# Feed-forward of an encoder layer: two passes instead of one, and the first sequence's up projection as seven block products

## The chip, the cores and the metric

One core of one Trainium2 chip runs the whole program in one launch. The metric is device time in microseconds (us), the median of three runs: 2488.31 us for the kernel before (2484.97 to 2488.56). TensorE is PE in the profile (PEld its weight loads), VectorE is DVE, ScalarE is ACT, GpSimd is POOL, SyncE is SP and issues the DMAs.

## The reference, cut to what matters

Two sequences (1024 and 512 tokens, model width 1024) go through the same encoder layer: attention, cross attention, and the gated feed-forward network, which alone is changed. All data are fp32.

```python
D_FF = 2816
h = _rmsnorm(x, norm_ffn_g)
u = jnp.einsum('bsd,df->bsf', h, w_up)              # width 2 * 2816
up = jnp.pad(u, ((0, 0), (1, 1), (0, 0)))
u = up[:, :-2] * conv_w[0] + up[:, 1:-1] * conv_w[1] + up[:, 2:] * conv_w[2] + conv_b
a, b = jnp.split(u, 2, axis=-1)
x = x + jnp.einsum('bsf,fd->bsd', jax.nn.silu(a) * b, w_down)
return _rmsnorm(x, final_norm_g)
```

## The kernel before, in words

Every operand of a matmul is held as two halves of type fp32r: `hi` (the value rounded) and `lo` (the rest). A product is three matmuls, hi by hi, hi by lo and lo by hi, each of 128x128 stationary by 512 moving columns. So each weight is split by POOL in two steps, a TENSOR_SCALAR that writes hi (L1683) and a TENSOR_TENSOR that subtracts (L1685), and each activation by ACT (hi) and DVE (lo).

The last phase, `rest_phase`, runs the output projection, the cross attention, its output projection, and from 1384.5 us of the span the feed-forward. Its steps up to there are in an order that a planner (`rest_plan`) writes out from costs and due times. The feed-forward is a loop over 22 groups of 128 hidden channels (`groups`, with `body` on each engine; a group has a gate unit s = 0 and a value unit s = 1). All 1536 tokens go together: the three chunks of 512 tokens of unit s fill three PSUM banks (`up_bank`), 8 k-steps of three matmuls each (`up`, L1719). `woven` lays the 24 down products of the group before (`down`, L1852, two banks `down_bank`) between the up products of the same iteration: a list of (up, down) steps that PE and DVE both follow. DVE adds each down product onto the rows `x` (`add`, L2081).

The up product of a unit is read out of PSUM in place: ACT applies the middle tap and the bias (L1957), DVE the two shifted taps (`conv_part`, L2071, one input in PSUM), ACT the silu (L1961), DVE the product of gate and value (L2102), ACT its hi half (L1963), DVE its lo half (L2104). Weights come by SP (`load`, L1598) into one staging buffer per kind. The last group is cut into three chunks (`END_PARTS`), and its down products are merged with those of the group before (L1894), followed by the final norm of each row tile (L2125, L1999, L2129, L1709, then L1990 and L1705, or L2137) and the stores.

## Time and profile before

| | kernel before |
|---|---|
| median of 3 runs | 2488.31 us |
| the profiled execution, whole | 2487.8 us |
| its span in the trace | 2486.0 us |
| mean granted TensorE clock | 0.995 |
| PE busy | 2432.8 us (98%) |
| DVE busy | 1477.4 us (59%) |
| POOL busy | 904.9 us (36%) |
| ACT busy | 823.2 us (33%) |

Busy is the union of the times in which an engine has an instruction in flight. A matmul of 512 columns is in flight for 0.39 us, but the next one starts much sooner, so the work of PE is read from the distance between starts, not from durations. The 1.8 us between the profiled execution and its span lie around the program.

### The profile page before, as it was taken

What the parts mean: (1) busy time and instruction counts of PE and PEld (TensorE: products, weight loads), DVE (VectorE), ACT (ScalarE), POOL (GpSimd) and SP (SyncE); (2) the same over time, 40 slices, a digit from 0 to 9 for tenths busy, and PEclk for the clock granted to TensorE, in tenths of its full rate; (3) what the DMA queues carried; (4) which work ended last, traced back from release to release, by engine and by line L of the source; (5) the groups of instructions that cost most, each with busy time, mean ns of one, the idle gap of its engine ahead of it and who ended that gap; (6) DMA issues with size and microseconds to landing.
All of it is one profiled execution on the core that took longest, in us unless ns stands there. A gap on an engine that the chain in (4) does not pass through costs nothing.

```text
span 2486.0 us, 34448 instructions
## 1 busy us (share of the span) xinstructions
PE 2432.8 (98%) x12666; PEld 2100.7 (85%) x12666; DVE 1477.4 (59%) x2149; ACT 823.2 (33%) x1498; POOL 904.9 (36%) x1234
## 2 busy tenths in 40 slices
PE   7999999999999989999999999999999999999997
PEld 6999999998998878888888888888888888888886
DVE  7536666788889963333434355555555555555555
ACT  4335555555778841133322211111111111111114
POOL 5453645598878520242400221122122212121223
PEclk9999999999999999999999999999999999999999
DMA  8743434432212162211434401010001100110102
GB/s 298 240 171 124 154 136 157 155 134 98 76 62 82 32 203 85 93 68 60 144 117 138 186 26 34 25 42 28 31 25 42 34 25 28 40 34 25 34 26 102
DMA packets 83379, 224.60 MB, mean 90 GB/s; under 512 B 8000, under 2 KB 43200, under 8 KB 72768
## 3 DMA queue, kind: packets, MB, share of 16 engines
q1 hardware_dynamic: 81968, 222.69, 26.0%
q8 instruction: 70, 1.15, 0.2%
q10 hardware_dynamic: 1296, 0.39, 0.1%
q14 instruction: 45, 0.37, 0.0%
HBM read 174.82 MB, written 48.23 MB: 90 GB/s over the span
## 4 chain that ended last, share of the span: by engine, by line
PE 63%; DVE 1%; issue 0%; POOL 0%; DMA 0%; ACT 0%; POOLq 0%; SPq 0%; DVEq 0%; ACTq 0%
PE r_bank L1719 29%; PE r_bank L1852 13%; PE r_bank L1748 11%; PE r_bank L1781 5%; PE r_bank L1894 1%; PE r_bank L1800 1%; PE r_bank L1829 1%; PE r_bank L1763 1%; PE r_bank L1812 0%; DVE r_x_rows L2137 0%; DMA o_raw<-o_scratch 0%; POOL r_w_lo L1685 0%; DVE r_prob L2051 0%; POOL r_w_hi L1683 0%; DVE r_conv L2119 0%
## 5 line engine op out<-in xcount | busy, mean ns | idle before, releaser
L2081 DVE TENSOR_TENSOR r_x_rows<-r_bank,r_x_rows 128x512 f32<-128x512 f32 x480 | 331.0, 690 | 356.8 <-PE r_bank L1852 356.8
L1719 PE MATMUL r_bank<-r_h_hi,r_w_hi 128*128 128x512 f32 x1056 | 411.0, 389 | 1.2 <-POOL r_w_lo L1685 1.2
L1719 PE MATMUL r_bank<-r_h_lo,r_w_hi 128*128 128x512 f32 x1056 | 410.8, 389 | 0.0
L1719 PE MATMUL r_bank<-r_h_hi,r_w_lo 128*128 128x512 f32 x1056 | 410.8, 389 | 0.0
L1683 POOL TENSOR_SCALAR r_w_hi<-r_stage 128x1024 fp32r<-128x1024 f32 x63 | 66.5, 1055 | 800.0 <-PE r_bank L1852 486.7
L832 PE MATMUL t_proj<-t_w_hi,t_hbuf 128*128 128x384 f32 x1056 | 311.1, 348 | 0.7 <-DVE t_hbuf L1075 0.5
L1957 ACT ACTIVATE r_conv<-r_bank,r_tap 128x1536 f32<-128x1536 f32 x42 | 68.8, 1637 | 630.7 <-PE r_bank L1719 630.7
L1719 PEld LDWEIGHTS r_bank<-r_h_hi,r_w_hi 128*128 128x128 f32 x1056 | 198.2, 188 | 42.7 <-POOL r_w_lo L1685 1.6
L1719 PEld LDWEIGHTS r_bank<-r_h_hi,r_w_lo 128*128 128x128 f32 x1056 | 198.2, 188 | 41.2
L1719 PEld LDWEIGHTS r_bank<-r_h_lo,r_w_hi 128*128 128x128 f32 x1056 | 198.2, 188 | 41.1
L1129 DVE TENSOR_REDUCE t_max_neg<-t_scores 128x1 f32<-128x1024 f32 (+1 forms) x192 | 197.7, 1037 | 33.2 <-PE t_scores L863 32.6
L996 ACT ACTIVATE t_prob<-t_scores,t_max_neg 128x1024 f32<-128x1024 f32 (+1 forms) x192 | 187.2, 976 | 67.9 <-DVE t_max_neg L1129 64.1
L2071 DVE SCALAR_TENSOR_TENSOR r_conv<-r_bank,r_tap,r_conv 128x1023 f32<-128x1023 f32 (+1 forms) x168 | 167.8, 1010 | 57.3 <-ACT r_conv L1957 55.7
L832 PEld LDWEIGHTS t_proj<-t_w_hi,t_hbuf 128*128 128x128 f32 x1056 | 196.3, 190 | 3.5 <-issue 0.7
L1149 DVE TENSOR_TENSOR t_pt_lo<-t_turn,t_pt_hi 128x512 fp32r<-128x512 f32 x240 | 163.1, 685 | 47.2 <-ACT t_pt_hi L1005 44.7
L1852 PE MATMUL r_bank<-r_w_hi,r_g_hi 128*128 128x512 f32 x480 | 188.7, 393 | 1.3
L1852 PE MATMUL r_bank<-r_w_lo,r_g_hi 128*128 128x512 f32 x480 | 186.8, 389 | 0.0
L1852 PE MATMUL r_bank<-r_w_hi,r_g_lo 128*128 128x512 f32 x480 | 186.8, 389 | 0.0
L832 PE MATMUL t_proj<-t_w_lo,t_hbuf 128*128 128x384 f32 x528 | 178.9, 339 | 0.0
L1005 ACT CAST t_pt_hi<-t_turn 128x512 fp32r<-128x512 f32 x240 | 139.4, 587 | 97.8 <-PE t_turn L876 85.3
L1685 POOL TENSOR_TENSOR r_w_lo<-r_stage,r_w_hi 128x1024 fp32r<-128x1024 f32 x63 | 151.6, 2406 | 5.3
L876 PE MATMUL t_turn<-ident,t_prob 128*128 128x128 f32 x960 | 142.8, 274 | 5.7 <-DVE t_ms L1156 2.4
(234 smaller groups left out, 5154.6 us busy)
## 6 DMA issues: line engine op xcount, KB each, us to landing
t_hbuf<-split_x SPq DMA_DIRECT2D x60, 1024.0 KB, 4.8
r_stage<-in_w_up_units SPq DMA_DIRECT2D x44, 512.0 KB, 3.3
split_x<-t_hbuf SPq DMA_DIRECT2D x12, 1024.0 KB, 4.9
r_stage<-in_w_down SPq DMA_DIRECT2D x22, 512.0 KB, 3.3
t_stage<-in_w_in_units SPq DMA_DIRECT2D x6, 1536.0 KB, 7.0
t_xkv_raw<-in_w_xkv_heads SPq DMA_DIRECT2D x16, 512.0 KB, 6.4
t_x_raw<-in_x_turned SPq DMA_DIRECT2D x12, 512.0 KB, 8.3
h_raw<-mix_scratch SPq DMA_DIRECT2D x12, 512.0 KB, 8.2
```

The lines of the kernel that those rows point to most:

```text
L832: ins = nc.tensor.matmul(proj_bank(i), l, r[:, k, :], start=(k == 0 and j == 0), stop=(k == KT - 1 and j == 2))
L876: ins = nc.tensor.transpose(ps_t[:, slot, kk * 2 * P + qt * P:kk * 2 * P + (qt + 1) * P], prob[:, n % PSLOTS, keys], ident[:, :])
L996: nc.scalar.activation(prob[:, n % PSLOTS, 0:p.keys], ps_s[:, n % 2, 0:p.keys], ACT.Exp, bias=max_neg[:, n % COLS:n % COLS + 1], accum_out ...
L1005: nc.scalar.copy(pt_hi[:, n % 2, :], ps_t[:, slot, :]).then_inc(pthi_done, 1)
L1129: nc.vector.tensor_reduce(max_neg[:, n % COLS:n % COLS + 1], ps_s[:, n % 2, 0:p.keys], AX.X, ALU.max, negate=True).then_inc(max_done, 1)
L1149: nc.vector.tensor_tensor(pt_lo[:, n % 2, :], ps_t[:, slot, :], f32(pt_hi[:, n % 2, :]), ALU.subtract).then_inc(ptlo_done, 1)
L1685: nc.gpsimd.tensor_tensor(w_lo[s][:, :], stage[s][:, :], f32(w_hi[s][:, :]), ALU.subtract).then_inc(w_split[s], 1)
L1719: ins = nc.tensor.matmul(up_bank(s)[:, c * BANK:(c + 1) * BANK], l, r, start=(k == 0 and j == 0), stop=(k == KT - 1 and j == 2))
L1748: ins = nc.tensor.matmul(acc(t)[:, cols], l[:, k, :], r[:, cols], start=(k == 0 and j == 0), stop=(k == KT - 1 and j == 2))
L1852: ins = nc.tensor.matmul(down_bank(n), l, r, start=j == 0, stop=j == 2)
L2071: ins = nc.vector.scalar_tensor_tensor(conv[:, s, o], up_bank(s)[:, x_cols], tap[:, j, s:s + 1], conv[:, s, o], ALU.mult, ALU.add)
L2081: nc.vector.tensor_tensor(x[:, t, cols], down_bank(n), x[:, t, cols], ALU.add).then_inc(add_done, 1)
```

## The change

The feed-forward runs in two passes over the 22 groups.

First pass: the second sequence (512 tokens, "sample") alone. A group has 8 + 8 up products (one bank for each unit) and 8 down products; on PE the gate unit runs alone and the value unit is interleaved with the downs of the group before. In groups 1 to 4 DVE also forms sums of blocks of the first sequence's normed activations (`sum_step`), in groups 5 to 11 ACT and DVE split the seven block operands into halves (`low_step`), between the adds.

Second pass: the first sequence (1024 tokens, "prompt"). The up product of a group is a 2x2 by 2x2 block product: gate and value unit by halves of the model width on the weight side, halves of the width by the two chunks of 512 tokens on the other. Instead of eight block products of 4 k-steps it has seven, `w11, s2, s1, w12, s3, w22, s4`, in the Strassen-Winograd form. POOL forms the sums of weight blocks (5 sums of 512 columns per group) and splits seven weight operands of 512 columns and two halves of the down weight. Out of the products DVE forms the four results with four adds in which one input is a PSUM bank; they lie in SBUF (`value`, `gate`), so the shifted taps now have both inputs in SBUF. The gate's second chunk comes out last (product s4), so the gated activations are made in two parts: the first 384 tokens (`edge`) and, in the next group's time, the other 640 (`late`). The 16 downs of the group before are interleaved with products 3 to 6; down 0 waits for `edge_split`, down 3 for `late_split`. Group 21's downs are merged with group 20's at the end, as before.

Around it: the output projection of the cross attention takes its row tiles in another order (`XO_TILES`), so that the second sequence's tiles are ready earlier, and DVE makes no lo half for the first sequence's tiles. Everything is unrolled; the loop and its `tap` copies are gone. Loads of weight quarters are 256 KB instead of 512 KB. The diff, cut to its core:

```diff
--- before.py
+++ after.py
...
+PRODUCTS = ("w11", "s2", "s1", "w12", "s3", "w22", "s4")
+PARTNER = {"w11": "h11", "s2": "t2", "s1": "t1", "w12": "h21", "s3": "t3", "w22": "t4", "s4": "h22"}
+PRODUCT_BANK = {"w11": 2, "w12": 2, "s2": 3, "s3": 3, "s1": 0, "s4": 0, "w22": 1}
...
+XO_TILES = [0, 1, 2, 3, 8, 9, 10, 11, 4, 5, 6, 7]
...
+EDGE = 3 * P
+SUMS = 4
...
+            def halves(hi, lo, raw):
+                stepped(nc.gpsimd.tensor_scalar(hi[:, :], raw[:, :], 1.0, 1.0, ALU.mult, ALU.mult))
+                return nc.gpsimd.tensor_tensor(lo[:, :], raw[:, :], f32(hi[:, :]), ALU.subtract)
...
+            def s3_of(i):
...
+                slot_free(i, "s3", "s3")
+                raw = wop_raw["s3"]
+                stepped(nc.gpsimd.tensor_tensor(raw[:, :], w_rows["w11"][:, :], w_rows["w21"][:, :], ALU.subtract))
+                halves(wop_hi["s3"], wop_lo["s3"], raw).then_inc(op_ready, 1)
...
+            def s2_s1_of(i):
...
+                slot_free(i, "s2", "w22")
+                s1, s2 = wop_raw["s1"], wop_raw["s2"]
+                stepped(nc.gpsimd.tensor_tensor(s1[:, :], w_rows["w21"][:, :], w_rows["w22"][:, :], ALU.add))
+                nc.gpsimd.tensor_tensor(s2[:, :], s1[:, :], w_rows["w11"][:, :], ALU.subtract).then_inc(s2_summed, 1)
+                pool.wait_ge(s2_summed, i + 1)
+                halves(wop_hi["s2"], wop_lo["s2"], s2).then_inc(op_ready, 1)
+                halves(wop_hi["s1"], wop_lo["s1"], s1).then_inc(op_ready, 1)
...
+            def s4_of(i):
+                pool.wait_ge(op_done, done_at(i, "w12"))
+                raw = wop_raw["s4"]
+                nc.gpsimd.tensor_tensor(raw[:, :], w_rows["w12"][:, :], f32(wop_hi["s2"][:, :]), ALU.subtract).then_inc(s4_begun, 1)
+                pool.wait_ge(s4_begun, i + 1)
+                stepped(nc.gpsimd.tensor_tensor(raw[:, :], raw[:, :], f32(wop_lo["s2"][:, :]), ALU.subtract))
+                halves(wop_hi["s4"], wop_lo["s4"], raw).then_inc(op_ready, 1)
...
+            for i in range(1, FT):
+                if i < LAST:
+                    split(i + 1, 0)
+                split_down(i, 0)
+                if i < LAST:
+                    split(i + 1, 1)
+                split_down(i, 1)
...
+            for i in range(FT):
+                from_rows(i, "w22")
+                if i == 0:
+                    pool.wait_ge(s_mean, ST)
...
+                s4_of(i)
+                if i < LAST:
+                    from_rows(i + 1, "w11")
+                    s3_of(i + 1)
+                    s2_s1_of(i + 1)
+                    if i == 0:
+                        from_rows(i + 1, "w12")
+                        down_half(i, 0)
                     else:
...
+                        down_half(i, 0)
+                        from_rows(i + 1, "w12")
+                    down_half(i, 1)
...
+            for i in range(1, FT):
+                for k in range(KT):
+                    sample_up(i, 0, k)
+                for k in range(KT):
+                    sample_up(i, 1, k)
+                    sample_down(i - 1, k)
...
+                if k == 0:
+                    pe.wait_ge(op_ready, ready_at(i, name))
+                    if name == "w11":
+                        pe.wait_ge(*((c11_out, i) if i else (y_done, both)))
+                        if i == 0:
+                            pe.wait_ge(h_op_done, HK * len(H_OPERANDS))
+                    elif name == "s2" and i:
+                        pe.wait_ge(u_done, i)
+                    elif name == "s1":
+                        pe.wait_ge(*((c12_done, i) if i else (s_conv_done, 2 * LAST + 1)))
+                    elif name == "w12":
+                        pe.wait_ge(p1_out, i + 1)
+                    elif name == "s3":
+                        pe.wait_ge(v_done, i + 1)
+                    elif name == "w22":
+                        pe.wait_ge(*((c21_done, i) if i else (s_conv_done, 2 * FT)))
+                    elif name == "s4":
...
+            def prompt_down(i, n):
+                c, t = n // PTILES, n % PTILES
+                if t == 0:
+                    pe.wait_ge(wd_ready, 2 * i + c + 1)
+                    pe.wait_ge(edge_split, i + 1)
+                elif n == 3:
+                    pe.wait_ge(late_split, i + 1)
+                if P_DOWNS * i + n >= 4:
+                    pe.wait_ge(p_add, P_DOWNS * i + n - 3)
+                elif n == 0:
+                    pe.wait_ge(s_add, S_DOWNS * FT)
+                tile = slice(t * P, (t + 1) * P)
+                three(down_bank(n), g_hi[:, tile], g_lo[:, tile], wd_hi[c][:, :], wd_lo[c][:, :], True, True).then_inc(p_down, 1)
...
+            for i in range(FT):
+                for o, name in enumerate(PRODUCTS):
+                    for k in range(HK):
+                        product(i, name, k)
+                        if i == 0 and o == 2:
+                            sample_down(LAST, 2 * k)
+                            sample_down(LAST, 2 * k + 1)
+                        elif 0 < i < LAST and 2 <= o < 6:
+                            prompt_down(i - 1, HK * (o - 2) + k)
...
+                    act.wait_ge(c21_done, i + 1)
+                    mid(i, 1, whole, value[:, :], value_mid)
+                    act.wait_ge(edge_prod, i + 1)
+                    if i == LAST:
+                        act.wait_ge(op_done, done_at(LAST, "w11"))
+                    elif i:
+                        act.wait_ge(p_down, P_DOWNS * i)
+                    else:
+                        act.wait_ge(y_sent, 16 * ST)
+                    nc.scalar.copy((e_hi if i == LAST else g_hi)[:, edge], conv[:, 0, edge]).then_inc(edge_hi, 1)
...
+                for n in range(S_DOWNS if i else 0):
+                    if i == 1 and n == 0:
+                        dve.wait_ge(s_rows_loaded, 16 * ST)
+                        dve.wait_ge(h_hi_done, both)
+                    sample_add(i - 1, n)
+                    if n % 2 and 1 <= i <= SUMS:
+                        sum_step(i - 1, n // 2)
+                    elif n % 2 and SUMS < i <= SUMS + len(H_OPERANDS):
+                        low_step(i - SUMS - 1, n // 2)
+                sample_shifts(i, 1)
...
+            def gated(i, cols, silu, prod, hi_done, split_done):
+                dve.wait_ge(silu, i + 1)
+                dve.wait_ge(value_conv, i + 1)
+                nc.vector.tensor_tensor(conv[:, 0, cols], conv[:, 0, cols], conv[:, 1, cols], ALU.mult).then_inc(prod, 1)
+                dve.wait_ge(hi_done, i + 1)
+                hi, lo = (e_hi, e_lo) if i == LAST else (g_hi, g_lo)
+                nc.vector.tensor_tensor(lo[:, cols], conv[:, 0, cols], f32(hi[:, cols]), ALU.subtract).then_inc(split_done, 1)
...
+            for i in range(FT + 1):
+                if i:
+                    dve.wait_ge(op_done, done_at(i - 1, "s4"))
+                    dve.wait_ge(v_done, i)
+                    nc.vector.tensor_tensor(gate[:, second], one_bank(PRODUCT_BANK["s4"]), gate[:, second], ALU.add).then_inc(c12_done, 1)
+                    dve.wait_ge(late_mid, i)
+                    two_shifts(i - 1, 0, (slice(BANK, 2 * BANK), slice(BANK - 1, 2 * BANK - 1)),
+                               (slice(BANK - 1, 2 * BANK - 1), slice(BANK, 2 * BANK)), late_conv)
+                else:
+                    for n in range(S_DOWNS):
+                        sample_add(LAST, n)
+                if i < FT:
+                    dve.wait_ge(p1_out, i + 1)
+                    dve.wait_ge(op_done, done_at(i, "s2"))
+                    if i:
+                        dve.wait_ge(late_conv, i)
+                    nc.vector.tensor_tensor(gate[:, second], one_bank(PRODUCT_BANK["s2"]), value[:, second], ALU.add).then_inc(v_done, 1)
+                if i:
+                    gated(i - 1, rest, late_silu, late_prod, late_hi, late_split)
+                else:
...
+                if i < FT:
...
+                    prompt_adds(i - 1, 0, 10)
+                    dve.wait_ge(c11_out, i + 1)
+                    two_shifts(i, 0, (slice(1, BANK), slice(0, BANK - 1)), (slice(0, BANK - 1), slice(1, BANK)), edge_conv)
+                    if i == 0:
...
+                        dve.wait_ge(s_rstd, 1)
+                        sample_scale(0)
+                    prompt_adds(i - 1, 10, 11)
+                    dve.wait_ge(op_done, done_at(i, "s3"))
+                    if i:
+                        dve.wait_ge(value_conv, i)
+                    nc.vector.tensor_tensor(value[:, first], one_bank(PRODUCT_BANK["s3"]), value[:, second], ALU.add).then_inc(u_done, 1)
+                    dve.wait_ge(u_done, i + 1)
+                    dve.wait_ge(v_done, i + 1)
+                    nc.vector.tensor_tensor(value[:, second], one_bank(PRODUCT_BANK["s1"]), value[:, first], ALU.add).then_inc(c22_done, 1)
+                    if i == 0:
+                        for t in range(1, ST):
+                            sample_scale(t)
+                    prompt_adds(i - 1, 11, 15)
+                    dve.wait_ge(op_done, done_at(i, "w22"))
+                    dve.wait_ge(c22_done, i + 1)
+                    nc.vector.tensor_tensor(value[:, first], value[:, first], one_bank(PRODUCT_BANK["w22"]), ALU.subtract).then_inc(c21_done, 1)
+                    prompt_adds(i - 1, 15, 16)
+                    dve.wait_ge(value_mid, i + 1)
+                    two_shifts(i, 1, (slice(1, 2 * BANK), slice(0, 2 * BANK - 1)), (slice(0, 2 * BANK - 1), slice(1, 2 * BANK)), value_conv)
+                    gated(i, edge, edge_silu, edge_prod, edge_hi, edge_split)
...
```

## Rows read from the trace of the kernel before

**Rows 1.** The page, parts 1 and 4: busy times, and the chain by engine.
```profile
PE 2432.8 (98%) x12666; PEld 2100.7 (85%) x12666; DVE 1477.4 (59%) x2149; ACT 823.2 (33%) x1498; POOL 904.9 (36%) x1234
...
PE 63%; DVE 1%; issue 0%; POOL 0%; DMA 0%; ACT 0%; POOLq 0%; SPq 0%; DVEq 0%; ACTq 0%
```

**Rows 2.** Timeline of PE: start us, us, then the instruction; its first and two mid-loop ups.
```profile
1384.54 0.39 PE L1719 MATMUL r_bank<-r_h_hi,r_w_hi 128*128 128x512 f32 x1
...
2001.41 0.39 PE L1719 MATMUL r_bank<-r_h_lo,r_w_hi 128*128 128x512 f32 x1
...
2004.13 0.39 PE L1719 MATMUL r_bank<-r_h_lo,r_w_hi 128*128 128x512 f32 x1
```

**Rows 3.** Waits from 1350 us on: who waited for whom, us in total, times, longest.
```profile
PEld r_bank L1852 <- issue: 9.2, 19, 0.5
...
PE r_bank L1894 <- DVE r_x_rows L2125: 3.0, 1, 3.0
```

**Rows 4.** Groups by line and shape: busy us, mean ns of one, idle before.
```profile
L2081 DVE TENSOR_TENSOR r_x_rows<-r_bank,r_x_rows 128x512 f32<-128x512 f32 x480 | 331.0, 690 | 356.8 <-PE r_bank L1852 356.8
...
L2071 DVE SCALAR_TENSOR_TENSOR r_conv<-r_bank,r_tap,r_conv 128x1023 f32<-128x1023 f32 x84 | 107.3, 1277 | 56.5 <-ACT r_conv L1957 55.7
...
L2071 DVE SCALAR_TENSOR_TENSOR r_conv<-r_bank,r_tap,r_conv 128x511 f32<-128x511 f32 x84 | 62.3, 742 | 0.8
...
L2027 DVE SCALAR_TENSOR_TENSOR r_normed<-r_x_xo,r_stat,r_gain 128x1024 f32<-128x1024 f32 x12 | 15.4, 1286 | 8.0 <-POOL r_stat L1632 8.0
```

**Rows 5.** Single lines of POOL and ACT: duration ns min/median/max, first and last start.
```profile
L1663 POOL TENSOR_SCALAR wxo_hi<-wxo_raw x16: 617/618/664, 1200.7 to 1232.7; 128x512 fp32r<-128x512 f32 x16
...
L1666 POOL TENSOR_TENSOR wxo_lo<-wxo_raw,wxo_hi x16: 1277/1288/1302, 1201.4 to 1233.4; 128x512 fp32r<-128x512 f32 x16
...
L1957 ACT ACTIVATE r_conv<-r_bank,r_tap x42: 1636/1637/1637, 1402.1 to 2403.9; 128x1536 f32<-128x1536 f32 x42
...
L1976 ACT ACTIVATE r_conv<-r_bank,r_tap x6: 762/780/781, 2415.5 to 2438.0; 128x512 f32<-128x512 f32 x6
...
L1982 ACT ACTIVATE r_conv<-r_conv x3: 524/633/740, 2417.9 to 2435.0; 128x512 f32<-128x512 f32 x1, 128x384 f32<-128x384 f32 x1, 128x640 f32<-128x640 f32 x1
...
L1985 ACT CAST r_e_hi<-r_conv x3: 512/622/724, 2421.6 to 2441.3; 128x512 fp32r<-128x512 f32 x1, 128x384 fp32r<-128x384 f32 x1, 128x640 fp32r<-128x640 f32 x1
```

**Rows 6.** Single lines of DVE, both inputs in SBUF, in the same form.
```profile
L2011 DVE TENSOR_TENSOR o_lo<-o_raw,o_hi x12: 1220/1226/1226, 1237.9 to 1366.5; 128x1024 fp32r<-128x1024 f32 x12
...
L2102 DVE TENSOR_TENSOR r_conv<-r_conv x21: 1759/2330/2336, 1424.1 to 2409.8; 128x1536 f32<-128x1536 f32 x21
...
L2145 DVE TENSOR_TENSOR r_conv<-r_conv x3: 558/692/826, 2420.9 to 2440.5; 128x512 f32<-128x512 f32 x1, 128x384 f32<-128x384 f32 x1, 128x640 f32<-128x640 f32 x1
```

**Rows 7.** Timeline of POOL and DVE where such an operation meets a split.
```profile
2013.68 2.41 POOL L1685 TENSOR_TENSOR r_w_lo<-r_stage,r_w_hi 128x1024 fp32r<-128x1024 f32 x1
...
2015.37 2.33 DVE L2102 TENSOR_TENSOR r_conv<-r_conv 128x1536 f32<-128x1536 f32 x1
```

**Rows 8.** Timeline of DVE and POOL, 909 to 919 us, several in a row.
```profile
910.00 5.95 DVE L2011 TENSOR_TENSOR h_lo<-h_raw,h_hi 128x1024 fp32r<-128x1024 f32 x3
...
909.79 1.29 POOL L1645 TENSOR_TENSOR r_wxq_lo<-r_wxq_raw,r_wxq_hi 128x512 fp32r<-128x512 f32 x1
911.05 1.60 POOL L1642 TENSOR_SCALAR r_wxq_hi<-r_wxq_raw 128x512 fp32r<-128x512 f32 x1
912.73 2.13 POOL L1645 TENSOR_TENSOR r_wxq_lo<-r_wxq_raw,r_wxq_hi 128x512 fp32r<-128x512 f32 x1
914.84 1.59 POOL L1642 TENSOR_SCALAR r_wxq_hi<-r_wxq_raw 128x512 fp32r<-128x512 f32 x1
```

**Rows 9.** Stretches at the end: busy us by engine, granted clock, DMA; and the chain's last matmuls.
```profile
2445.00:2449.00 4.00, 4.00 (x12) 3.11 (x11) 1.45 (x3) 1.07 (x3) 0.55 (x1) 0.57 0.00 0
...
2443.68 32.70 PE r_bank L1894 x132
```

**Rows 10.** DMA issues by line: KB each, median us to landing.
```profile
r_stage<-in_w_up_units SPq DMA_DIRECT2D x44, 512.0 KB, 3.3
```

More of the change, by code:

```diff
@@ new lines, in rest_phase, with ready_at @@
+        edge_hi, late_hi, edge_split, late_split = sem("edge_hi"), sem("late_hi"), sem("edge_split"), sem("late_split")
+        p_rows_loaded, p_down, p_add = sem("p_rows_loaded"), sem("p_down"), sem("p_add")
+        last_gain, end_down, end_add, sum_done = sem("last_gain"), sem("end_down"), sem("end_add"), sem("sum_done")
+        last_mean, last_rstd, scaled, out_a, out_b, y_sent = (sem(n) for n in ("last_mean", "last_rstd", "scaled", "out_a", "out_b", "y_sent"))
+        def ready_at(i, name):
+            late = ("w22", "s4")
+            if name in late:
+                return NP * i + 6 + late.index(name)
+            return NP * i + 1 + (("w11", "s3", "s2", "s1", "w12") if i else ("w11", "s2", "s1", "w12", "s3")).index(name)
@@ L1612, in _ @@
[L1612 to L1618 removed]
+                        sp.wait_ge(pv_done, EB * XU)
+                    elif s == 2:
+                        for e in range(EB):
+                            sp.wait_ge(o_stored[CH - 1][e], 16 * X_HEADS)
@@ new lines, in three, with sample_down @@
+            def three(out, l_hi, l_lo, r_hi, r_lo, first, last, onto=False):
+                for j, (l, r) in enumerate(((l_hi, r_hi), (l_hi, r_lo), (l_lo, r_hi))):
+                    ins = nc.tensor.matmul(out, l, r, start=(first and j == 0), stop=(last and j == 2), skip_group_check=onto)
+                return ins
+            def sample_down(i, n):
+                t, c = n % ST, n // ST
+                if t == 0:
+                    pe.wait_ge(w_split[2], 2 * i + c + 1)
+                    pe.wait_ge(s_split, i + 1)
+                    if i == 0:
+                        pe.wait_ge(h_hi_done, both)
+                if S_DOWNS * i + n >= 4:
+                    pe.wait_ge(s_add, S_DOWNS * i + n - 3)
+                tile, cols = slice(t * P, (t + 1) * P), slice(c * BANK, (c + 1) * BANK)
+                three(down_bank(n), sg_hi[:, tile], sg_lo[:, tile], w_hi[2][:, cols], w_lo[2][:, cols], True, True).then_inc(s_down, 1)
```

670 lines of the change are left out of this document (393 added, 277 removed).

## Prediction

> **What bounds the kernel now.** I read the busy times and the chain first. PE is busy 98% of the span and holds 63% of the chain that ended last, every other engine 1% or less [rows 1]. Then the timeline of PE in the loop: 12 matmuls, from 2001.41 to 2004.13, take 2.72 us, so one takes 0.2267 [rows 2]. PE's part of the feed-forward runs from 1384.54 [rows 2] to 2443.68 + 32.70 = 2476.38 [rows 9], that is 1091.8 us. It holds 22 x (144 up + 72 down) = 4752 matmuls, 1077.2 us. The other 14.6 us are a wait of 3.0 before the last downs, 1.3 lost at the lower clock behind it (12 matmuls in 4.00 us instead of 2.7; granted clock 0.57, partly 1.2 GHz), the turns of the loop, where the weight load stood 9.2 us in 19 places [rows 3, 9], and small things. So this stage is matmuls back to back, and a matmul less is 0.2267 us less as long as everything else keeps up. The question is whether it does.
>
> **The matmuls.** After, a group has 48 + 24 for the second sequence and 7 x 4 x 3 = 84 products and 48 downs for the first: 204 instead of 216. 22 x 12 x 0.2267 = **59.8 us less**, 4488 matmuls in 1017.4 us. The unrolled program also drops the turns of the loop; of the 14.6 us I leave 4 standing.
>
> **What one shape costs.** POOL at 512 columns: hi 0.62, a subtraction or sum 1.29 [rows 5]. DVE: add out of PSUM 0.69; a shift 0.74 at 512 columns and 1.28 at 1023; product or lo half 0.83 at 640 and 0.56 at 384 [rows 4, 6]. ACT: tap and bias 0.78 at 512, 1.64 at 1536, so 1.21 at 1024; silu 0.74 and 0.52, hi half 0.72 and 0.51 at 640 and 384 [rows 5]. From the end of one engine's step to the next engine's start I take 0.04, and 0.2 from PE's nominal end.
>
> **POOL's load.** First-sequence group: 9 splits (1.91 each) and 5 sums (1.29) are 23.6 us, with 14 gaps of 0.08 behind a wait 24.7. PE has 132 matmuls, 29.9 us. Before it was three splits of 1024 in 49 us. DVE has 21 adds out of PSUM, 14.5, and ten operations with both inputs in SBUF: six shifts (4 x 0.74 + 2 x 1.28) and four of product and lo (2 x 0.83 + 2 x 0.56), 8.3 us. Each engine alone fits under 29.9.
>
> **But these ten and POOL exclude each other.** L2102, both inputs in SBUF, takes 1.76 at least but 2.33 in the median [rows 6]; it starts at 2015.37 while a POOL subtraction lasts until 2016.09, and ends 1.61 after that: it waited and gained only 0.15 by overlap [rows 7]. Several in a row alternate strictly: from POOL's end at 911.08 to DVE's third end at 915.95, 4.87 us hold three DVE operations of 1.22 and POOL's 0.62 and 1.29, whose rows are stretched to 1.60 and 2.13; the sum is 5.57, so a handover saves 0.14 [rows 5, 6, 8]. Operations with an input in PSUM don't show it: L2071 has a mean of 1277 beside POOL's splits [rows 4]. The change moves the shifts from PSUM to SBUF inputs and keeps POOL busy for most of the time. The Trainium skill, SBUF — State Buffer, section "Who interferes with whom", says that the port pair DVE and GpSimd share is an exclusive lock that the loser waits out fully. Read to the letter that is rival 5 below; the rows have an overlap, and I go by them.
>
> **One group in the steady state.** Time 0 is when product w22 of group i is seen. PE then has one down (to 0.5), s4 (3.2), w11 (5.9), s2 (8.6), and s1 with downs: down 3 of group i is due at 13.4. POOL at 0 starts the two sums, and everything that waits alternates (own time less 0.14 at each handover). c21 0.7, ACT's tap on both chunks 2.0; POOL's sums 2.7; shift 3.85; POOL hi 4.3; shift 5.5; POOL lo 6.6, which is operand s2, due at 5.9; product of the first 384 tokens 7.0; POOL hi 7.5; ACT hi 7.6; POOL lo 8.9; lo 9.3 (edge_split, due at 9.3); c12 10.0; ACT tap 10.8; shift 11.75 (behind POOL's down split); POOL hi 12.2; shift 12.8; silu 13.6; POOL lo 14.0; product of the 640 14.7; ACT hi 15.4; POOL lo 16.5; **lo 17.2 (late_split)**. Down 3 starts 3.8 us late. Without the exclusion the same steps end at about 12.6 and nothing is late. Behind down 3 PE queues all the rest of the group; DVE's adds 3 to 9 and then the first chunk's shifts, s3 and s2+s1 adds follow it, so that c21 is some 0.3 late at the next w22, and POOL, which has s4 (4.75 after w12 is done), w11, s3 to do before 0, is just in time. I take **4.0 us a group**, from group 1's down 3 to group 20's, 19 times: 76.
>
> **First pass.** 72 matmuls, 16.3 us; POOL 11, DVE up to 12.5. The chain from the last up product of the value unit to the first down: due 6.8 after it. Add 1.6, shifts 3.05, product behind POOL's 1024-column subtraction (2.4, to 3.75) 4.3, hi 4.9, lo behind the next split 6.7: just in time. In groups 1 to 11 a sum or low step stands before the shifts and waits for that subtraction too (to 4.3); shifts 5.8, product 6.7, hi 7.3, lo 8.15: 1.35 late. 11 x 1.35 = **15 us**; bounds 0 (the steps fall elsewhere) and 25.
>
> **Change of pass.** No row shows it; by the same prices. POOL's last down split and operand w11 start only when PE's loop is through: PE waits 4.5, then 2.4 for s2. DVE does 8 adds, the means, and the second sequence's four scalings (1.29) between the first results; POOL's rsqrt step stands before s4 and waits for ACT's four squares. s4 starts 2.5 late, c21 comes 8 behind, s2 of group 1 another 9.5, and group 1's down 3, due 34.7 after the first pass, starts at 57.8, behind the down weight, whose load waits for the stores. **23 us**, bounds 14 and 30. **The end.** Group 21 has no downs between its products, so w12 waits 2 for POOL, s4 2.4, and the last lo half comes 0.6 late, with small waits: 6; the last matmul to the end of the span stays 9.6, as before.
>
> **Hidden edits.** The ups of the second sequence start under the last norm as the first two chunks did: 10.9 us of matmuls cover the same steps. Weight loads of 256 KB are asked for at least 6 us before use, and 512 KB land in 3.3 [rows 10]. The new tile order and the lo halves left out touch DVE at 59% [rows 1]. I cost them at nothing; uncovered they are a few us.
>
> **Sum.** 1017.4 + 4 + 15 + 23 + 76 + 6 = 1141.4 against 1091.8: +49.6. Span 2486.0 + 49.6 = 2535.6, with the 1.8 around it 2537.4, and the median of the runs lies 0.5 above the profiled one: **2538 us**.
>
> **Rivals.** (1) *The exclusion doesn't act on these shapes, or the steps fall in POOL's gaps* (the other side). For it: ten operations of 8.3 and POOL's 24.7, less 20 handovers of 0.14, are 30.2, hardly more than PE's 29.9, so that only the order of the steps makes them late. Against: rows 7 and 8. Then no steady stall, no stall in the first pass, 14 and 4 at the seams: 1017.4 + 4 + 18 = 1039.4, 2436 us. The point from which it decides is 1.4 us a group: 1091.8 less 1017.4, 4, 15, 23 and 6 leaves 26.4 for 19 groups. (2) *Half of it*: 2 us a group and 8 in the first pass, 2493 us. (3) *The clock falls as well*: behind a wait of 3.0 the granted clock fell once [rows 3, 9]; waits of 1.6 to 3.8 a group could do so each time, at 1.3 to 1.7 us: 20 groups, 2564 to 2572. Against: in my timeline the wait splits into two or three smaller ones. (4) *Loads come late*: some 10 us more, 2548. (5) *No overlap at a handover*: the 16 handovers of the chain at 0.14 are 2.2 us a group, 19 x 2.2 = 42, 2580. Against: the overlap stands in rows 7 and 8.
>
> **How the numbers follow.** Forecast 0.57 (its own range 2505 to 2560: the bounds of the seams and the first pass, and 1 us a group either way), rival 1 0.10, rival 2 0.10, rival 3 0.15, rival 4 0.05, rival 5 0.03. The range of 8 in 10 is 2488 to 2575: rival 1 is left out, and a tenth at the edges. This kernel's runs differ by some 0.15%, so 0.2% (5 us) is about what can be told from no change. Faster by more than that: rival 1 and a little of 2, 0.13; within 0.04; slower 0.83.
>
> **What the profile would show.** Right: matmuls 264 fewer at the same spacing; DVE's two-SBUF rows in the second pass far above their shortest (1.28 to about 2.4), waits of PE's down line for `late_split` (DVE's lo half) and of s2's product for POOL, in each of 20 groups some 4 us; a group every 34 us. Wrong: groups every 30 us (rival 1), granted clock under 0.95 in the second pass (rival 3), waits that end with a DMA (rival 4), or DVE's adds as what PE waits for.

## The result, and the profile after

The changed kernel takes **2539.95 us** (median; 2539.73 to 2540.69) against 2488.43 of the kernel before in the same session: ratio 1.021, 95% interval 1.0193 to 1.0228. It is slower by 51.5 us. The profiled execution spans 2537.8 us with a mean granted clock of 0.991. The forecast was 2538.0, its range 2488 to 2575.

The page, parts 1 and 4, as in [rows 1]:

```profile
PE 2400.6 (95%) x12402; PEld 2047.8 (81%) x12402; DVE 1733.7 (68%) x2407; ACT 895.5 (35%) x1706; POOL 1554.1 (61%) x1779
...
PE 47%; DVE 9%; ACT 4%; issue 3%; POOL 2%; DMA 0%; DVEq 0%; ACTq 0%; POOLq 0%; SPq 0%
```

The 264 matmuls are gone (12666 to 12402) and the span grew all the same. PE's share of the chain fell from 63% to 47%, DVE's rose from 1% to 9%. POOL is busy for 1554 us instead of 905.

A group of the second pass, two windows of one group each. Columns: window, length, busy us of PE, PEld, DVE, ACT, POOL with instructions, granted clock, DMA share, GB/s:

```profile
2001.58:2035.32 33.74, 31.10 (x134) 24.48 (x133) 26.91 (x33) 6.31 (x9) 28.34 (x23) 1.00 0.14 47
2035.32:2069.06 33.74, 31.11 (x134) 24.48 (x133) 26.91 (x32) 6.31 (x9) 28.38 (x23) 1.00 0.14 47
```

The second window repeats the first to 0.04 us: a steady state of 33.74 us in which neither DVE (26.9) nor POOL (28.3) is full, although the durations of both include the time that an instruction stands in its row and waits for the other engine. 132 matmuls are 29.92, so a group loses 3.82. PE's timeline shows where, in that group (the bracket is PE's idle time and what ended it; single matmuls at their nominal distance have none):

```profile
2008.20 0.50 PE L2023 MATMUL r_bank<-r_t_hi,r_s_hi 128*128 128x512 f32 x1 [0.54 <-POOL r_s_lo L1793]
...
2011.57 0.47 PE L2023 MATMUL r_bank<-r_t_hi,r_s_hi 128*128 128x512 f32 x1 [0.35 <-DVE r_rows L2405]
...
2012.72 0.50 PE L2023 MATMUL r_bank<-r_wd_hi,r_g_hi 128*128 128x512 f32 x1 [0.22 <-POOL r_wd_lo L1793]
...
2018.63 0.50 PE L2023 MATMUL r_bank<-r_wd_hi,r_g_hi 128*128 128x512 f32 x1 [1.53 <-DVE r_g_lo L2383]
```

These are product s2 (waits for its operand), s1 (waits until DVE has emptied its bank, L2405), down 0 (waits for the down weight's lo half) and down 3 (waits for `late_split`, L2383). Taken from start to start, less the 0.2267 of a matmul [rows 2], they lose 0.70, 0.51, 0.39 and 1.69, together 3.3; the rest of the 3.8 is in smaller steps. The same wait over the whole pass, 1350 us to the end (who waited for whom, us in total, times, longest):

```profile
PE r_bank L2023 <- DVE r_g_lo L2383: 29.1, 19, 1.5
```

Now the path to down 3 in that group, DVE and POOL (start us, us). L2318 is a shift, L2380 the product, L2383 a lo half; L1792 and L1793 are POOL's hi and lo:

```profile
2003.09 1.29 POOL L1825 TENSOR_TENSOR r_s_raw<-r_s_raw,r_rows_w 128x512 f32<-128x512 f32 x1
2003.64 3.37 DVE L2318 SCALAR_TENSOR_TENSOR r_conv<-r_rows,r_taps,r_conv 128x1023 f32<-128x1023 f32 x2 [0.69 <-ACT r_conv L2204]
...
2004.47 1.47 POOL L1792 TENSOR_SCALAR r_s_hi<-r_s_raw 128x512 fp32r<-128x512 f32 x1
2006.02 2.13 POOL L1793 TENSOR_TENSOR r_s_lo<-r_s_raw,r_s_hi 128x512 fp32r<-128x512 f32 x1
2007.12 1.45 DVE L2380 TENSOR_TENSOR r_conv<-r_conv 128x384 f32<-128x384 f32 x1
...
2016.62 1.27 POOL L1793 TENSOR_TENSOR r_wd_lo<-r_wd_raw,r_wd_hi 128x512 fp32r<-128x512 f32 x1
2016.86 1.71 DVE L2383 TENSOR_TENSOR r_g_lo<-r_conv,r_g_hi 128x640 fp32r<-128x640 f32 x1 [0.80 <-ACT r_g_hi L2220]
```

The alternation of [rows 8] is there. POOL's hi and lo, 0.62 and 1.29 by themselves [rows 5], stand at 1.47 and 2.13 beside DVE's two shifts, and the product of 384 columns at 1.45 where the form took 0.56 [rows 6]. The last line is the one that decides. The lo half of 640 columns needs 0.83, but it starts 0.24 us behind a POOL subtraction, lasts 1.71, and down 3 starts 0.06 after its end at 2018.57.

### The profile page after: what moved, and what is told of

Same layout as the page of the kernel before. It is cut to its first block, busy times and chain, and to the rows that moved or that the text cites. A ratio compares the mean times of both kernels' runs of the same rounds, so it can differ in the third digit from the quotient of the medians.

```text
span 2537.8 us, 33971 instructions
## 1 busy us (share of the span) xinstructions
PE 2400.6 (95%) x12402; PEld 2047.8 (81%) x12402; DVE 1733.7 (68%) x2407; ACT 895.5 (35%) x1706; POOL 1554.1 (61%) x1779
## 4 chain that ended last, share of the span: by engine, by line
PE 47%; DVE 9%; ACT 4%; issue 3%; POOL 2%; DMA 0%; DVEq 0%; ACTq 0%; POOLq 0%; SPq 0%
PE r_bank L2023 19%; PE r_bank L1929 10%; PE r_bank L1900 9%; PE r_bank L1962 5%; DVE r_conv L2318 4%; DVE r_conv L2380 2%; ACT r_conv L2204 2%; DVE r_g_lo L2383 1%; PE r_bank L1981 1%; PE r_bank L2010 1%; PE r_bank L1944 1%; ACT r_conv L2218 1%; ACT r_g_hi L2220 1%; DVE r_rows L2448 1%; DVE r_rows L2405 1%
## 5 line engine op out<-in xcount | busy, mean ns | idle before, releaser
L2388 DVE TENSOR_TENSOR r_x_p<-r_bank,r_x_p 128x512 f32<-128x512 f32 x320 | 211.3, 685 | 70.9 <-PE r_bank L2023 67.7
L2318 DVE SCALAR_TENSOR_TENSOR r_conv<-r_rows,r_taps,r_conv 128x511 f32<-128x511 f32 (+1 forms) x132 | 167.6, 1269 | 40.5 <-ACT r_conv L2204 38.2
L1778 POOL TENSOR_TENSOR r_w_lo<-r_stage,r_w_hi 128x1024 fp32r<-128x1024 f32 (+1 forms) x86 | 166.1, 1931 | 7.2
L2023 PE MATMUL r_bank<-r_wd_hi,r_g_hi 128*128 128x512 f32 x336 | 135.3, 403 | 34.3 <-DVE r_g_lo L2383 29.1
L897 PE MATMUL t_acc<-t_pt_hi,t_v_hi 128*128 128x256 f32 x480 | 138.4, 305 | 7.3 <-DVE t_pt_lo L1149 5.7
L862 PE MATMUL t_scores<-t_qk 128*128 128x512 f32 x320 | 136.0, 425 | 1.5 <-ACT t_prob L996 1.5
L1900 PE MATMUL r_bank<-r_hs_hi,r_w_hi 128*128 128x512 f32 x352 | 137.2, 390 | 0.0
L1900 PE MATMUL r_bank<-r_hs_hi,r_w_lo 128*128 128x512 f32 x352 | 137.0, 389 | 0.0
L1900 PE MATMUL r_bank<-r_hs_lo,r_w_hi 128*128 128x512 f32 x352 | 137.0, 389 | 0.0
L1793 POOL TENSOR_TENSOR r_s_lo<-r_s_raw,r_s_hi 128x512 fp32r<-128x512 f32 x88 | 130.3, 1481 | 7.3
```

The source lines that it names most:

```text
L1778: nc.gpsimd.tensor_tensor(lo, raw, f32(hi), ALU.subtract).then_inc(w_split[s], 1)
L1900: ins = nc.tensor.matmul(one_bank(s), l, r, start=(k == 0 and j == 0), stop=(k == KT - 1 and j == 2))
L2023: ins = nc.tensor.matmul(out, l, r, start=(first and j == 0), stop=(last and j == 2), skip_group_check=onto)
L2318: return nc.vector.scalar_tensor_tensor(out, src, tap_of(j, s, i), out, ALU.mult, ALU.add)
L2388: nc.vector.tensor_tensor(x_p[:, t, cols], down_bank(n), x_p[:, t, cols], ALU.add).then_inc(p_add, 1)
```

## Experiments

**1. GpSimd's work without its reads.** The second pass in which every sum and every split on POOL is replaced by fills (`fill(x, n)`: n instructions that write zeros into x):

```diff
-                stepped(nc.gpsimd.tensor_scalar(hi[:, :], raw[:, :], 1.0, 1.0, ALU.mult, ALU.mult))
-                return nc.gpsimd.tensor_tensor(lo[:, :], raw[:, :], f32(hi[:, :]), ALU.subtract)
+                stepped(fill(f32(hi[:, :]), 1))
+                return fill(f32(lo[:, :]), 2)
...
-                stepped(nc.gpsimd.tensor_tensor(raw[:, :], w_rows["w11"][:, :], w_rows["w21"][:, :], ALU.subtract))
+                stepped(fill(raw[:, :], 2))
```

> GpSimd's work of the second pass keeps its place, its order and about its length, but reads nothing: every conversion to a high half is one fill with zeros, every difference, sum and low half two fills. So the weights of the first sequence's up projection and of its down projection are left out (zeros), and the output is not the reference's. Theory (GpSimd's instructions and VectorE's with two inputs in SBUF exclude each other): VectorE's rows fall to the durations without a neighbour (1023 columns 1.28 us, 640 columns about 0.8), the steady group falls from 33.7 us to 30.0 to 30.5, the whole to 2455 to 2485 us. Rival (GpSimd is late by the length of its own chain of steps, VectorE by its own): the group stays at 33 to 34 us if the fills take as long as what they replace, the whole at 2530 to 2545. If fills exclude VectorE as well, the rows stay long and the run tells only that.

Measured: 2452.37 us, ratio to the kernel before 0.9855 (0.9838 to 0.9871), 2.6 below the theory's range; a group takes 29.92 us. The groups by line of the window 1839.57 to 2345.40, which is 15 groups of the changed kernel, that kernel first:

```profile
L2318 DVE SCALAR_TENSOR_TENSOR r_conv<-r_rows,r_taps,r_conv 128x1023 f32<-128x1023 f32 x30 | 50.1, 1669 | 10.9 <-ACT r_conv L2204 10.3
...
L2383 DVE TENSOR_TENSOR r_g_lo<-r_conv,r_g_hi 128x640 fp32r<-128x640 f32 x15 | 25.8, 1719 | 11.9 <-ACT r_g_hi L2220 11.9
```

and with fills:

```profile
L1793 POOL MEMSET r_s_raw<- 128x512 f32 x85 | 44.9, 529 | 106.8 <-PE r_bank L2028 104.9
...
L2323 DVE SCALAR_TENSOR_TENSOR r_conv<-r_rows,r_taps,r_conv 128x1023 f32<-128x1023 f32 x34 | 43.6, 1284 | 12.3 <-ACT r_conv L2209 11.7
...
L2388 DVE TENSOR_TENSOR r_g_lo<-r_conv,r_g_hi 128x640 fp32r<-128x640 f32 x17 | 14.0, 825 | 13.5 <-ACT r_g_hi L2225 13.5
```

DVE's rows fell from 1669 to 1284 and from 1719 to 825 ns, and PE has no wait left in the window: its 132 matmuls are 29.92 us. But a difference was now 2 x 0.53 instead of 1.29 us, so POOL's chain was shorter as well, and the rival was not quite out.

**2. The same with a chain that is not shorter.** The edit, against experiment 1:

```diff
             def fill(out, times):
+                stepped(nc.gpsimd.memset(out[:, 0:96 if times == 1 else 224], 0.0))
                 for _ in range(times - 1):
```

> As the run with fills in the second pass (the same work left out: zeros for the weights there, so the output is not the reference's), but each conversion is a fill of 512 and one of 96 columns, each difference, sum and low half two of 512 and one of 224, so that GpSimd's chain is longer by its own time than the one of the changed kernel without neighbours (more than 23.6 us in a group). Theory (exclusion): VectorE's rows stay at their lengths without a neighbour, the group stays within 1 us of 29.9, the whole at 2450 to 2475. Rival (the first run with fills won because its chain was 4 us shorter): the group goes back to 32 us or more, the whole to 2500 or more.

Measured: 2477.16 us (one run), 2.2 above the theory's range and far from the rival's 2500. A conversion is now 0.53 + 0.18 = 0.71 us, and a sum or subtraction 2 x 0.527 + 0.286 = 1.34. A group has 9 x 0.71 + 14 x 1.34 = 25.2 us of POOL in 60 instructions, against 23.6 in 23 for the real ones without a neighbour. Groups by line, same window:

```profile
L2324 DVE SCALAR_TENSOR_TENSOR r_conv<-r_rows,r_taps,r_conv 128x1023 f32<-128x1023 f32 x32 | 41.1, 1284 | 11.6 <-ACT r_conv L2210 11.0
...
L2389 DVE TENSOR_TENSOR r_g_lo<-r_conv,r_g_hi 128x640 fp32r<-128x640 f32 x17 | 14.0, 826 | 13.5 <-ACT r_g_hi L2226 13.5
```

and the only thing that PE waits for there:

```profile
PE r_bank L2029 <- POOL r_wd_lo L1795: 10.3, 16, 0.7
```

A group takes 30.87 us (one stall of 0.8 each, at down 0). So the length of POOL's chain by itself costs at most 0.95 us a group, and the exclusion accounts for at least the other 2.9 of the 3.8. DVE's rows don't notice the fills, which write and don't read: what excludes DVE goes with POOL's reading. The Trainium skill, SBUF — State Buffer, section "Who interferes with whom", says just this of a DVE instruction with two SBUF inputs: it contends with a GpSimd instruction that reads SBUF, "not with one that only writes it". These two runs agree.

**3. One step of the first pass moved.**

```diff
+                    if n == S_DOWNS - 1:
+                        continue
                     if n % 2 and 1 <= i <= SUMS:
                         sum_step(i - 1, n // 2)
...
                 nc.vector.tensor_tensor(sg_lo[:, :], s_conv[:, 0, :], f32(sg_hi[:, :]), ALU.subtract).then_inc(s_split, 1)
+                if 1 <= i <= SUMS:
+                    sum_step(i - 1, HK - 1)
+                elif SUMS < i <= SUMS + len(H_OPERANDS):
+                    low_step(i - SUMS - 1, HK - 1)
```

> Only the last of the four sum or low steps that a group of the first pass takes on is moved, from behind the group's eighth sample addition to behind the low half of the gated tile. Theory (that step, 0.9 us with two inputs in SBUF and a GpSimd instruction ahead of it, is what makes the gated tile late for the next group's first down product): the 11 stalls of 1.5 us go, the whole falls by 13 to 18 us, to 2522 to 2527. Rival (the four steps as a whole fill the group's slack, wherever they stand): the stalls stay within 0.5 us of 1.5, the whole within 5 us of 2540.

Measured: 2525.28 us, 14.7 less; ratio to the kernel before 1.0149 (1.0132 to 1.0166). Stretches of the first pass, changed kernel first:

```profile
1350.00:1740.00 390.00, 374.86 (x1650) 305.02 (x1649) 272.03 (x338) 84.14 (x125) 242.21 (x168) 1.00 0.30 99
```

```profile
1350.00:1740.00 390.00, 390.00 (x1719) 318.12 (x1718) 280.36 (x351) 86.99 (x129) 251.57 (x174) 1.00 0.31 103
```

PE runs 69 matmuls more in the same 390 us, without a pause: 15.6 us. All 11 stalls are gone, although DVE does the same work. It was the place of the step. What the step waited for stands in the trace of the changed kernel, in one of the 11 groups:

```profile
1430.97 2.39 POOL L1778 TENSOR_TENSOR r_w_lo<-r_stage,r_w_hi 128x1024 fp32r<-128x1024 f32 x1
...
1431.00 2.91 DVE L2338 TENSOR_TENSOR r_t_raw<-r_t_raw,r_h_rows 128x512 f32<-128x512 f32 x1
```

The sum starts 0.03 us behind POOL's subtraction of 1024 columns and ends 0.55 after it; it took 2.91 us, while in the run with the step moved a sum of the same shape took 0.68 with POOL idle (start 1426.80). The shifts, which read PSUM, stood behind it; in that run they start at once and take their usual 1.52 for two beside the same subtraction.

**4. POOL's order in the second pass.**

```diff
+                if i < LAST:
+                    from_rows(i + 1, "w11")
                 s4_of(i)
                 if i < LAST:
-                    from_rows(i + 1, "w11")
                     s3_of(i + 1)
...
```

> Only GpSimd's order in the second pass is changed: the split of the next group's w11 goes ahead of this group's s4, in the 4.0 us in which GpSimd waits for the w12 product. Theory (GpSimd's train of 23 instructions behind that wait is on the path): the stalls of TensorE before s2 (0.70) and before down product 0 (0.39) go, VectorE's late path starts beside less GpSimd work, the group falls by 1.1 to 2.5 us, the whole by 20 to 45, to 2495 to 2520. Rival (the late path of VectorE sets the period by its alternation with whatever GpSimd instruction is there): the group falls by less than 0.5 us, the whole to 2530 or more.

Measured: 2541.61 us, 1.7 more than the changed kernel, no gain. The rival was right in size. POOL's waits in the window (15 groups), changed kernel first:

```profile
POOL r_s_raw L1833 <- PE r_bank L2023: 60.2, 15, 4.0
```

```profile
POOL r_s_raw L1835 <- PE r_bank L2026: 30.6, 15, 2.1
...
POOL r_s_raw L1826 <- PE r_bank L2026: 24.6, 15, 1.7
```

Its wait of 4.0 us before s4 became 2.1, and others appeared further on: 0.8 before s3 and 1.7 before the sums for s1 and s2, which wait until product w22 has freed s1's slot. POOL's chain from there to operand s2 starts when PE says so, however early POOL is.

**5. Edits 3 and 4 together.**

> Both edits together, the moved low step of the first pass and GpSimd's new order in the second. The two passes don't overlap, so the theory expects the sum of both gains: 2480 to 2505 us. If it is above 2510, one of them gave back what it won at the change of pass.

Measured: 2527.05 us, 22 above the expected range: the gain of edit 3 and nothing of edit 4. The expectation had counted on edit 4; the sum of the two measured changes, 14.7 less and 1.7 more, is 2526.9.

**6. s2 without that slot.** On top of edit 3, and with w11 split ahead of s4 as in edit 4:

```diff
+                stepped(nc.gpsimd.tensor_tensor(s3[:, :], w_rows["w11"][:, :], w_rows["w21"][:, :], ALU.subtract))
+                nc.gpsimd.tensor_tensor(s2[:, :], w_rows["w22"][:, :], s3[:, :], ALU.subtract).then_inc(s2_summed, 1)
...
+                slot_free(i, "s1", "w22")
+                stepped(nc.gpsimd.tensor_tensor(s1[:, :], w_rows["w21"][:, :], w_rows["w22"][:, :], ALU.add))
```

> On top of the moved low step (2525), GpSimd forms s2 of the next group as w22 - (w11 - w21) as soon as s3 is formed, without waiting for the w22 product to free the slot of s1; w11 is split ahead of s4, s1 comes last. Theory: the stalls before s2 (0.70) and before down product 0 (0.39) go, the others stay: the group falls by 1.1, the whole to 2500 to 2508. Rival (VectorE's late path, which alternates with any GpSimd instruction, sets the period): its stall grows by what the others lose, the whole over 2518.

Measured: 2522.14 us, 3.1 less than edit 3 alone: the rival again. PE's waits in the window:

```profile
PE r_bank L2040 <- DVE r_g_lo L2406: 22.6, 15, 1.5
PE r_bank L2040 <- DVE r_rows L2428: 22.4, 15, 1.5
```

The waits for POOL are gone, but the wait for DVE's c12 add (L2428) rose from 0.35 to 1.5 a group, and the one for `late_split` stayed at 1.5. Of that, 0.7 is PE's coming earlier by the stall that it no longer has before s2, and 0.3 is DVE's coming later: its two long shifts, in alternation with POOL, took 3.67 where they had taken 3.37.

**7. The down products one product later.** On top of edit 3; VectorE's additions move accordingly:

```diff
-                        elif 0 < i < LAST and 2 <= o < 6:
-                            prompt_down(i - 1, HK * (o - 2) + k)
+                        elif 0 < i < LAST and 3 <= o < 7:
+                            prompt_down(i - 1, HK * (o - 3) + k)
```

> On top of the moved low step (2525), the 16 down products of a group of the first sequence stand beside w12, s3, w22 and s4 and not beside s1, w12, s3 and w22, so each is due 2.7 us later; VectorE's additions move with them. Theory (what stops TensorE is the due time of VectorE's split against its length in alternation with GpSimd; 1.69 + 0.39 of the 3.8 us in a group hang on the down products): group 33.7 to about 31.7, the whole to 2480 to 2495. Rival (VectorE's and GpSimd's excluded time together fill the group): the stalls before s2 and s1 grow by what the others lose, the group stays over 33, the whole over 2515.

Measured: **2458.7 us**, 66.6 less than edit 3 alone and ratio 0.9881 (0.9864 to 0.9897) to the kernel before. That is far more than expected, in the theory's direction. PE's waits in the window, and two groups by line:

```profile
PE r_bank L2023 <- DVE r_g_lo L2389: 3.2, 16, 0.2
```

```profile
L2318 DVE SCALAR_TENSOR_TENSOR r_conv<-r_rows,r_taps,r_conv 128x512 f32<-128x512 f32 x34 | 43.5, 1279 | 15.6 <-ACT r_conv L2204 15.0
...
L2389 DVE TENSOR_TENSOR r_g_lo<-r_conv,r_g_hi 128x640 fp32r<-128x640 f32 x16 | 27.9, 1743 | 12.7 <-ACT r_g_hi L2220 12.7
```

A group is 30.44 us. The rows of DVE are as stretched as ever (1743 ns for 640 columns, and 1279 at 512 where the changed kernel had 946), and PE hardly waits: the exclusion goes on and costs next to nothing. Why more than the 2.1 us that I had put on the two down stalls? Beside s1 there are no downs any more, but there are beside s4. From the end of w22, when POOL's chain to s2 and DVE's to the first 384 columns start, PE now has one down, 24 matmuls of s4 with its downs and 12 of w11 ahead of s2, 39 in all; in the changed kernel it had one down, s4 and w11, 27. So s2 and everything behind it is due 12 x 0.2267 = 2.7 us later, and the stalls before s2 and s1 go too (one stall of 0.36 a group is left). I had moved the downs in my expectation and not what stands around them.

**8. All three.** Edits 3, 6 (with 4 in it) and 7, and operand w12 split ahead of the down halves:

> All three: moved low step, s2 formed early (and w12 split ahead of the down halves), down products later by one product. Theory: nothing in a steady group is late any more, the group is 30.0 to 30.6 us, the whole 2448 to 2470 us, below the kernel before. Rival (the excluded time of both engines, about 31.5 us in a group, is the bound): group 31.5 to 32.5, the whole 2484 to 2503.

Measured: **2450.08 us**, ratio 0.9848 (0.9832 to 0.9865). The window of the 15 groups:

```profile
1839.57:2345.40 505.83, 505.83 (x2233) 418.83 (x2232) 413.58 (x524) 106.78 (x152) 471.25 (x390) 1.00 0.17 53
```

This is in the theory's range. PE is busy without a gap: 2233 matmuls, 16.9 groups of 29.9 us, where the changed kernel got through 15, with POOL at 93% and DVE at 82% of the window. The rival, that the excluded time of both engines adds up to the bound, fell: edit 6, with the order of w12, is worth 8.6 us here and was worth 3.1 alone, when the stalls of the down products stood behind it.

**9. The form of the small step at the end.** On top of the last kernel:

```diff
-                nc.vector.scalar_tensor_tensor(last_stat[:, m, 0:1], last_stat[:, m, 0:1], EPS, last_stat[:, m, 1:2],
-                                               ALU.add, ALU.add).then_inc(last_mean, 1)
+                nc.vector.tensor_scalar(last_stat[:, m, 0:1], last_stat[:, m, 0:1], last_stat[:, m, 1:2], EPS,
+                                        ALU.add, ALU.add).then_inc(last_mean, 1)
```

> On top of all three edits (2450). Only the form of the mean step at the very end (128x1) is changed: one instruction with one input in SBUF and a scalar for each partition, in place of one with two inputs in SBUF. Theory: the steps that stood at 1.58 to 1.63 us beside GpSimd's gain product of 2.4 us take 0.2 us or less like the others, for the form and not the size decides; but the next instruction with two inputs waits for the same gain product, so the whole gains only 1 to 3 us. Rival (the step waits for something else at the end of the kernel, the squares' sums of ScalarE): it stays at 1.6 us in three of eight places.

Measured: 2449.85 us, no change (expected 1 to 3 less). The single line, changed kernel first (durations in ns, min/median/max):

```profile
L2461 DVE SCALAR_TENSOR_TENSOR r_last_stat<-r_last_stat x8: 143/160/1621, 2512.7 to 2530.4; 128x1 f32<-128x1 f32 x8
```

```profile
L2486 DVE TENSOR_SCALAR r_last_stat<-r_last_stat x8: 194/214/215, 2422.3 to 2438.7; 128x1 f32<-128x1 f32 x8
```

One element for each partition took up to 1.62 us with two inputs in SBUF, and 0.215 at most with one: the form decides, not the size. It gained nothing, since the instruction with two inputs that comes next waits for the same POOL product, and POOL's power step now falls behind that one:

```profile
2430.16 2.41 POOL L1899 TENSOR_TENSOR r_x_p<-r_x_p,r_gain_p 128x1024 f32<-128x1024 f32 x1 [0.33 <-ACT r_x_p L2268]
...
2432.07 1.58 DVE L2493 SCALAR_TENSOR_TENSOR r_x_p<-r_x_p,r_last_stat,r_gain_p 128x1024 f32<-128x1024 f32 x1
...
2432.54 1.53 POOL L1903 TENSOR_TENSOR r_last_stat<-r_last_stat,minus_half 128x1 f32<-128x1 f32 x1
```

The power step takes 0.55 without a neighbour and 1.53 here.

**10. One engine for the last tiles.** As 9, and `scale(PTILES - 2)` on VectorE ahead of `scale(PTILES - 1)`, in place of ScalarE's and GpSimd's two steps.

> As e_mean, and the scaling of the last tile but one is VectorE's too, as one instruction, in place of ScalarE's 1.13 and GpSimd's 2.34 us. Theory: VectorE's last scaling is 1.27 us in place of 3.37, with 1.27 for the other ahead of it: another 0.5 to 1.5 us.

Measured: 2446.44 us, 3.4 less (expected 0.5 to 1.5). VectorE's last two scalings:

```profile
2438.39 2.48 DVE L2493 SCALAR_TENSOR_TENSOR r_x_p<-r_x_p,r_last_stat,r_gain_p 128x1024 f32<-128x1024 f32 x2 [0.32 <-POOL r_last_stat L1903]
```

Two in 2.48 us. The expectation had compared them with the 3.37 that the last scaling takes beside POOL's gain product in the kernel before, in the changed one and in run 8. But in run 9 the two had changed places, and it was POOL's product that waited and ended last:

```profile
2439.71 1.28 DVE L2493 SCALAR_TENSOR_TENSOR r_x_p<-r_x_p,r_last_stat,r_gain_p 128x1024 f32<-128x1024 f32 x1 [0.84 <-POOL r_last_stat L1903]
...
2440.42 2.77 POOL L1899 TENSOR_TENSOR r_x_p<-r_x_p,r_gain_p 128x1024 f32<-128x1024 f32 x1 [0.74 <-ACT r_x_p L2268]
```

What fell away is this path over three engines (POOL's power step, ScalarE's 1.15, POOL's product). From the end of the last matmul to the end of the span it was 14.3 us in run 9 and is 11.2 now.

**11. The order at the change of pass.** As 10, and in the first group the split of the next w11 goes ahead of the step that waits for the second sequence's sums.

> As e_tail, and in the first group of the second pass GpSimd's split of the next w11 goes ahead of the step on the second sequence's sums, for which it waits 2.4 us. Theory: s4 of that group is ready 2 to 3 us sooner, its stall of 6.4 falls to 3.5 to 4.5, and what follows it comes as much sooner: the whole falls by 2 to 5 us against e_tail. Rival (GpSimd has a fixed amount of work to do up to the third group, and stalls merely move): the sum of the stalls between 1740 and 1835 stays within 1 us.

Measured: 2445.88 us, ratio 0.9823 (0.9806 to 0.9839), 0.6 less than run 10, which is no more than the runs of one kernel differ by, and not the 2 to 5 expected. The stall before s4 fell from 6.37 to 2.68, further than the theory said. A new one of 2.57 appeared before s2 of the next group, and the one before its s1 rose from 2.62 to 3.32; those before down 0 (1.37) and before the s1 after it (0.97) went. The sum of the stalls fell from 16.0 to 13.3 (not the rival's). But the clock took more than half of that back. Stretches, run 10 first:

```profile
1770.00:1780.00 10.00, 3.78 (x15) 2.82 (x14) 9.97 (x8) 0.53 (x1) 9.75 (x6) 0.88 0.90 351
1780.00:1790.00 10.00, 9.86 (x34) 7.55 (x33) 7.26 (x6) 2.37 (x3) 9.58 (x8) 0.78 0.71 238
1790.00:1800.00 10.00, 6.47 (x27) 5.02 (x28) 7.74 (x7) 2.13 (x4) 9.67 (x9) 1.00 0.08 26
```

```profile
1770.00:1780.00 10.00, 7.48 (x28) 5.71 (x27) 9.76 (x9) 0.60 (x2) 6.95 (x5) 0.86 0.95 379
1780.00:1790.00 10.00, 6.17 (x25) 4.43 (x23) 7.19 (x6) 2.86 (x4) 9.58 (x8) 0.97 0.72 258
1790.00:1800.00 10.00, 8.27 (x24) 6.59 (x25) 7.00 (x6) 1.57 (x3) 9.58 (x10) 0.66 0.08 26
```

In run 10, 76 matmuls in these 30 us are 20.11 us busy, 2.9 more than 76 x 0.2267; here 77 are 21.92, 4.5 more. The granted clock now falls behind the last two stalls, to 0.66, and 1.6 of the 2.7 us are lost that the shorter stalls had won. Neither theory named this; it is shown for this place only.

## Why the prediction was right, point by point

- *The matmuls*: 264 fewer at the same spacing, 59.8 us. As predicted.
- *First pass, 15 us*: 11 stalls of 1.54, 17 us. That the place of the last sum or low step makes them is shown by run 3, and its row of 2.91 us, which ends 0.55 after POOL's long subtraction, shows that this is what it waits for. The predicted loss was 1.35 a group.
- *Steady state, 4.0 a group*: 3.82, 19 times, 72.6 us instead of 76. The exclusion as its cause is shown by runs 1 and 2, and that it costs only where a due time is missed by runs 7 and 8. The end of the chain, `late_split`, was predicted 17.2 us after product w22 and came after 17.0. In detail the timeline was less exact. It had down 3 late by 3.8 in all, 0.7 of it lost at s2 already; measured were 0.70 at s2 to the point, 0.51 at s1, 0.39 at the down weight and 1.69 at down 3. The due time of down 3 moves with every stall ahead of it, so the sum held while its parts didn't. (The results of the products are formed with five adds out of PSUM, as the prediction's 21 adds count them, and not with four as stated ahead of it.)
- *Change of pass, 23 us*: stalls of 4.71, 2.68, 0.91, 8.03 and 1.17 (predicted 4.5 for w11, 2.5 for s4, 9.5 for s2 of group 1), together 17.5. The rest is the clock, which the sum hadn't priced there. Two stretches:

```profile
1762.00:1769.00 7.00, 5.64 (x13) 4.32 (x14) 1.17 (x2) 0.74 (x2) 6.74 (x6) 0.52 0.00 0
...
1800.00:1810.00 10.00, 4.73 (x11) 3.77 (x12) 7.45 (x6) 2.53 (x4) 9.58 (x8) 0.50 0.37 136
```

  Behind the stalls of 4.7 and 8.0 the granted clock is 0.52 and 0.50, the 1.2 GHz level: 13 matmuls took 5.64 us of busy time instead of 2.95, and 11 took 4.73 instead of 2.49, so 4.9 us. Together 22.4. The term was right in size by an error in each direction: stalls too long by a few us (s2 of group 0 didn't wait at all, since PE ran at half speed ahead of it), and no price for the clock.
- *The end, 6 us*: stalls of 0.71, 0.52, 1.04 and 2.25 and about 1.6 at a clock of 0.57, 6.1. But "the last matmul to the end of the span stays 9.6" was wrong: it is 13.2. DVE's last add starts 4.0 us after the end of the last matmul, where before it started 0.02 after it. Two of DVE's small steps wait for POOL's gain products there, one of them here:

```profile
2520.83 2.40 POOL L1882 TENSOR_TENSOR r_x_p<-r_x_p,r_gain_p 128x1024 f32<-128x1024 f32 x1
...
2521.62 1.62 DVE L2461 SCALAR_TENSOR_TENSOR r_last_stat<-r_last_stat 128x1 f32<-128x1 f32 x1 [0.19 <-ACT r_junk_p L2259]
```

  In the kernel before the longest such row has 671 ns; I had not looked at it. The last scaling, 3.37 us beside the product, stands in both kernels and adds nothing. How the 3.6 us divide is not shown: run 9 shortened the small steps and won nothing, and run 10 won 3.4 by another path.
- *The sum*: 17 + 72.6 + 22.4 + 6.1 + 3.6 = 121.7 us of losses, less 59.8, less the 14.6 of other losses of before, is 47.3 against 51.8 measured between the spans; the 4.5 that are missing are near the "4 left standing" of the forecast. That the whole came within 2 us of the forecast is in part luck: the first pass (2.0) and the end (3.6) were priced too low and the steady state (3.4) too high.
- *Rivals*: 1 (steps fall in POOL's gaps) did not come true here, but its reason, that 30.2 us of excluded work is hardly more than PE's 29.9 and "only the order of the steps makes them late", is what runs 7 and 8 turned into a faster kernel. 2436 was its forecast; 2446 was reached (run 11). 2, half of the exclusion, had 2 us a group and 8 in the first pass, against 3.8 and 17. 3 fell: the clock stays at 1.00 in the steady state although a stall of 1.7 comes every group. 4: no wait of PE in the second pass ends with a DMA. 5: with no overlap at handovers the group would have lost 6, it lost 3.8.

What stays open: how much of the change of pass can be removed. The one edit that was run there (11) moved stalls and clock at once.
